# An eight-core encoder layer on Trainium2: local-attention chunks taken one step at a time, one swap in the start-up loads, and twenty extra matmuls in the first loop

## The chip, the cores and the metric

One Trainium2 chip, 8 cores on two dies. Each core computes one of the 8 sequences of the batch; nothing is exchanged between cores. The metric is the device time in microseconds (us) of the slowest core. Engines: PE is TensorE (PEld its weight loads), ACT ScalarE, DVE VectorE, POOL GpSimd, SP SyncE; the last two issue DMAs.

## The reference

```python
h = x @ w_in                                   # 2048 x 1024 by 1024 x 4608
qa, ka, va, za, qb, kb, vb, zb, ga, gb = split(h)
ya = windowed_sink_attention(qa, ka, va, sink) # local: |t-s| <= 128, ALiBi, sink logit
ya = (ya * silu(za)) @ w_proj_a
qh, kh = rope(rms_norm(qb)), rope(rms_norm(kb))
yb = softmax(qh @ kh.T / 8) @ vb               # global, 8 query heads on 2 kv heads
yb = (yb * silu(zb)) @ w_proj_b
y = (sigmoid(ga + b_a) * ya + sigmoid(gb + b_b) * yb) @ w_out
out = layer_norm(2 ** 0.25 * x + y)
```

A sequence has 2048 tokens, the model width is 1024, a head is 64 wide, and each mixer has 8 query heads and 2 key/value heads.

## The kernel before

The tensors that the profile names: `XT` is x transposed in bf16, in four quarters of 512 tokens with 8 slices of 128 channels (k slices, index kc) each. `WS` holds the weights of q, k, v of the global mixer and k, v of the local one; it lies in the memory called `SZ`, so the profile calls it SZ there. `PT` holds exponentiated scores, in 6 slots, a step each. `BIASC` is the local mixer's table of decays (mask included), by which `PT` is multiplied. `G` holds gates, `T` also merged branches and rows of x.

**Start.** DMAs on POOL's queue bring `WS` slice by slice and quarter 0 of `XT` two slices at a time (lines 315 to 328), then the identity and quarter 1 in two halves (330, 331). A DMA that reads the key of an earlier one waits on POOL until that one has landed, so such keys pace the issue. The **first loop** (701 to 705) goes over kc: for blocks 0 to 2 of 128 tokens two matmuls each (384 and 512 columns), then `ka_first` (512 columns). It needs slice kc of both `WS` and `XT`. Then `s_mm(3)` and, for t from 4 to 15, transposes of block t-4 (line 405), the projection of block t, and the rotary and norm work of block t-2 on DVE, ACT and POOL.

**Main loop** (965 to 994). The attention is a list of items (mixer B or A, head pair c, window Q of 512 queries). A B item has 16 steps, one for each block of 128 keys; an A item has 3. A step has score matmuls into a pair of PSUM banks, one exp of 128x1024 on ACT into a `PT` slot, for A one multiply by `BIASC` on DVE, and value matmuls (pv) into bank 4. Two bank pairs alternate, so the scores of step k wait for the exp of step k-2. Sums of the exponentials (ones matmuls) go to bank 5. `batches` packs steps in pairs, a single one where the step is the last of an A item: a B item is 8 batches, an A item a pair and a single.

One turn of the loop, for batch i, writes out this order: scores and exps of further batches, until at least two steps beyond batch i are begun; pv of batch i (and ones, after four steps or at the end of an item); at the end of an item the epilogue's first product `O`; the multiplies by `BIASC` of batch i+1; at the end of an item the transpose `TR`; some **fill** matmuls (`pump`); a tick, at which postponed DVE work runs: one tick after an item's end `rec` (reciprocal, four small copies, transpose `R`), two ticks after it the product into `SZ`. Each engine runs its part of the list in order.

**Fill** is all the rest: projections of local queries, gates and silu paths, the branch projections and the output projection, in groups of 4 or 8 matmuls in banks 6 and 7 alternately, each emptied by ACT or DVE, together with the layer norm. Per window of the loop it has about 176 (first), 320, 352 and 256 matmuls. They are dealt to the batches by weight (lines 863 to 870): 0.9 for a single, 1.5 for a last batch of an item with an A item behind it, 1.0 otherwise. The order of items is B B B A A B A A in window 0, BABABABA in 1, ABABABAB in 2 and 3. Behind the loop the fill of the last window runs by itself, and then the last norm.

Of the kernel before, what the change touches and what calls it, by code (L numbers as in the profile page):

```python
# [170 lines left out]
def build_program():  # L171
# [17 lines left out]
    with contextlib.ExitStack() as es:  # L189
        def sb(name, shape, dt):  # L190
            return es.enter_context(nc.sbuf_tensor(name, shape, dt))

        XT = sb("XT", [128, 4, 8, 512], BF16)
# [31 lines left out]
        PS = es.enter_context(nc.psum_tensor("PS", [128, 8, 512], F32))  # L225
        PSF = PS[:].rearrange("p b f -> p (b f)")

        WS = SZR[:].bitcast(BF16).rearrange("p (k c) -> p k c", k=8)
# [16 lines left out]
        RG_SZ, RG_W, RG_T = ("RG", "SZ"), ("RG", "W"), ("RG", "T")  # L245
# [7 lines left out]
        def pk(b, h=None):  # L253
            return [("PS", b, 0), ("PS", b, 1)] if h is None else [("PS", b, h)]

        def mm(out, lhsT, rhs, start, stop, reads, writes, skip=False):
            s.op("pe", lambda e: e.matmul(out, lhsT=lhsT, rhs=rhs, start=start, stop=stop, skip_group_check=skip),  # L257
                 reads=reads, writes=writes)

        def act(out, in_, func, reads, writes, bias=None, scale=None):  # L260
            kw = {}
            if bias is not None:
                kw["bias"] = bias
            if scale is not None:
                kw["scale"] = scale
            s.op("act", lambda e: e.activation(out=out, in_=in_, func=func, **kw), reads=reads, writes=writes)  # L266
# [8 lines left out]
        def dma(eng, out, in_, reads, writes):  # L275
            s.op(eng, lambda e: e.dma_start(out=out, in_=in_), reads=reads, writes=writes, dma=True)  # L276
# [8 lines left out]
        def load_ws(kc, after=()):  # L285
            dma("pool", WS[:, kc, :], d_ws[:, kc * 1024:(kc + 1) * 1024], [RG_SZ] + list(after), [("WS", kc)])

        def load_xt(n, k0, k1, after=()):
            dma("pool", XT[:, n, k0:k1, :], d_xT[n, :, k0 * 512:k1 * 512].rearrange("p (k t) -> p k t", t=512),
                list(after), [("XT", n, k) for k in range(k0, k1)])  # L290
# [32 lines left out]
        load_ws(4, [("WS", 0)])  # L323
        load_xt(0, 4, 6, [("WS", 1)])
        load_ws(5, [("WS", 2)])
        load_ws(6, [("XT", 0, 2)])
        load_xt(0, 6, 8, [("WS", 3)])
        load_ws(7, [("WS", 4)])
        dma("pool", IDENT[:], d_ident, [], [("IDENT",)])
        load_xt(1, 0, 4, [("WS", 5)])  # L330
        load_xt(1, 4, 8, [("WS", 6)])
        act(ESINK[:], CV[:, 16:20], AF.Exp, reads=[("CV",)], writes=[("ESINK",)])
        s.op("dve", lambda e: e.tensor_scalar_mul(out=CVH[:], in0=CV[:, 0:16], scalar1=0.5),
             reads=[("CV",)], writes=[("CVH",)])
# [9 lines left out]
        def s_part(t, kc, bk, part):  # L344
            n, tt_ = t // 4, t % 4
            xs = XT[:, n, kc, tt_ * 128:(tt_ + 1) * 128]
            rd = [("XT", n, kc), ("WS", kc), RG_SZ]
            if part == 0:
                mm(PS[:, bk, 0:512], xs, WS[:, kc, 0:512], kc == 0, kc == 7, rd, pk(bk))
            elif part == 1:  # L350
                mm(PS[:, bk + 1, 0:384], xs, WS[:, kc, 512:896], kc == 0, kc == 7, rd, pk(bk + 1))
            else:
                mm(PS[:, bk + 1, 384:512], WS[:, kc, 896:1024], xs, kc == 0, kc == 7, rd, pk(bk + 1))
# [6 lines left out]
        def ka_first(kc):  # L360
            mm(PS[:, 4, :], WS[:, kc, 896:1024], XT[:, 0, kc, :], kc == 0, kc == 7,
               [("XT", 0, kc), ("WS", kc), RG_SZ], pk(4))

        def s_copy(t, bk):
            act(VX[:, t, :], PS[:, bk + 1, 128:384], AF.Copy, pk(bk + 1), [("V", t)])
            if t > 3:
                act(KA[:, t * 128:(t + 1) * 128], PS[:, bk + 1, 384:512], AF.Copy, pk(bk + 1), [("KA", t)])
# [333 lines left out]
        for kc in range(8):  # L701
            for t in range(3):
                s_part(t, kc, sbk[t], 1)
                s_part(t, kc, sbk[t], 0)
            ka_first(kc)
        s_copy(0, sbk[0])
        act(KA[:, 0:512], PS[:, 4, :], AF.Copy, pk(4), [("KA", t) for t in range(4)])
        s_copy(1, sbk[1])
# [133 lines left out]
        def make(its):  # L842
            steps = []
            for kind, c, Q in its:
                n = 16 if kind == "B" else 3
                for i in range(n):
                    steps.append(Step(None, kind, c, Q, i, i == n - 1))
            return steps

        def batches(steps):  # L850
            out, i = [], 0
            while i < len(steps):
                n = 1 if steps[i].last else 2
                out.append(steps[i:i + n])
                i += n
            return out

        windows = [[("B", 0, 0), ("B", 1, 0), ("B", 2, 0), ("A", 0, 0), ("A", 1, 0), ("B", 3, 0), ("A", 2, 0), ("A", 3, 0)]]
        for Q in range(1, 4):
            windows.append([(kd, c, Q) for c in range(4) for kd in ("BA" if Q == 1 else "AB")])  # L860
        all_b = [(w, bt) for w, its in enumerate(windows) for bt in batches(make(its))]
        
        def weight_of(i):
            bt = all_b[i][1]
            if len(bt) == 1:
                return 0.9
            return 1.5 if i + 1 < len(all_b) and all_b[i + 1][1][0].kind == "A" and bt[-1].last else 1.0

        weights = [weight_of(i) for i in range(len(all_b))]
        left_b = [sum(x for x, (w, _) in zip(weights, all_b) if w == k) for k in range(4)]  # L870

        def start_batch(bt):
# [210 lines left out]
```

How the kernel before makes its waits and increments, by code:

```python
        def run_stream(e, engobj):  # L116
            waited = {}
            def wait(semkey, sem, val):
                if waited.get(semkey, 0) >= val:
                    return
                waited[semkey] = val
                engobj.wait_ge(sem, val)
            for o in streams[e]:
                for d in o.deps:
                    p = ops[d]
                    if p.dma:
                        wait(("d",) + p.dsem, dsems[p.dsem[0]][p.dsem[1]], p.dval)
                    elif self._need_sync(p, o):
                        wait(("e", p.eng), esem[p.eng], p.cnt)
                if o.dma:
                    sem = dsems[o.dsem[0]][o.dsem[1]]
                    if o.dval > 16:
                        wait(("d",) + o.dsem, sem, o.dval - 16)
                    o.fn(engobj).then_inc(sem, 16)
                else:
                    ins = o.fn(engobj)
                    if o.signal:
                        ins.then_inc(esem[e], 1)
            if e in DMA_POOL:
                last = {}
                for o in streams[e]:
                    if o.dma:
                        last[o.dsem] = o.dval
                for k, v in last.items():
                    wait(("d",) + k, dsems[k[0]][k[1]], v)
```

## Time and profile before

| | us |
|---|---|
| median of 3 runs (lowest, highest) | 697.12 (695.37, 737.5) |
| the profiled execution: its time | 696.03 |
| its span, slowest core (all cores) | 694.5 (690.5 to 694.5) |
| PE, ACT, DVE, POOL busy | 615.0, 391.8, 371.9, 125.4 |

All rows are of core 1, its slowest. Times count from the span's start. A bracket behind a line of a timeline tells how long the engine stood idle before it and what ended that.

### The profile page before, as it was taken

To read this page: it belongs to the slowest core of one execution; us is meant where nothing else is said; L and a number is where in the kernel's file an instruction comes from. 1 tells how busy PE (TensorE), PEld (TensorE's weight loads), DVE (VectorE), ACT (ScalarE), POOL (GpSimd) and SP (SyncE) were. 2 spreads that over 40 slices of the span, in tenths; PEclk is the share of its full clock that TensorE was granted. 3 is DMA by queue.
4 is the path that set the end of the run, shared out by engine and by line. 5 is a ranking of instruction groups with operands and counts; after the bars stand their busy time and mean duration, and the time that the engine had idled before them with its cause. 6 is when DMAs were issued, how large, how long until landed. Compare 5 with 4: busy or idle time off the path is not lost.

```text
span 694.5 us, 13589 instructions; the slowest of 8 cores (690.5 to 694.5 us)
## 1 busy us (share of the span) xinstructions
PE 615.0 (89%) x4440; PEld 237.7 (34%) x4440; DVE 371.9 (54%) x740; ACT 391.8 (56%) x515; POOL 125.4 (18%) x193
## 2 busy tenths in 40 slices
PE   3799988997989999999699799989897999999991
PEld 1356532332333333333233233333332333344440
DVE  2288833326281626265926626174758253579467
ACT  0156678784866566766356275756674767631210
POOL 3268541010011111001111111001110101112012
PEclk9999999998999999999999899999999999999996
DMA  9969739564046432344672543245674224418403
GB/s 136 148 119 126 87 70 157 87 119 58 1 47 107 61 49 39 41 59 76 79 148 49 97 77 48 40 62 92 127 178 103 50 33 61 62 39 202 63 1 121
DMA packets 26772, 57.60 MB, mean 83 GB/s; under 512 B 3024, under 2 KB 5200, under 8 KB 26448
## 3 DMA queue, kind: packets, MB, share of 16 engines
q0 software_dynamic: 21520, 39.36, 41.7%
q1 hardware_dynamic: 5184, 17.38, 7.8%
q8 instruction: 37, 0.61, 0.4%
q14 instruction: 31, 0.25, 0.1%
HBM read 86.65 MB, written 8.39 MB: 137 GB/s over the span
## 4 chain that ended last, share of the span: by engine, by line
PE 73%; DVE 9%; issue 7%; ACT 5%; DMA 4%; POOL 1%; DVEq 0%; ACTq 0%; POOLq 0%
PE PS L257 73%; ACT PT L266 4%; DMA SZ<-ws 2%; DVE PT L269 2%; DMA XT<-xT 1%; DVE T L272 1%; ACT G L266 1%; DVE D L827 1%; DVE WR L269 1%; DVE G L272 1%; DVE STT L574 1%; DVE TR L816 1%; PE PS L405 1%; DVE QB L272 1%; DVE O L269 0%
## 5 line engine op out<-in xcount | busy, mean ns | idle before, releaser
L266 ACT ACTIVATE PT<-PS 128x1024 bf16<-128x1024 f32 (+1 forms) x304 | 292.1, 1018 | 118.4 <-PE PS L257 116.5
L257 PE MATMUL PS<-XT,WROT 128*128 128x512 bf16 x896 | 224.7, 388 | 7.3 <-DVE G L272 6.3
L257 PEld LDWEIGHTS PS<-XT,WROT 128*128 128x128 bf16 x896 | 79.2, 99 | 127.3 <-issue 53.6
L276 POOL DMA_DIRECT2D WROT<-wg x100 | 53.4, 536 | 321.5 <-PE PS L257 320.0
L257 PE MATMUL PS<-PT,VX 128*64 128x512 bf16 (+3 forms) x688 | 97.8, 370 | 9.9 <-DVE PT L269 8.8
L257 PE MATMUL PS<-QB,KB 64*128 64x512 bf16 x512 | 83.6, 387 | 19.2 <-ACT PT L266 18.8
L272 DVE SCALAR_TENSOR_TENSOR G<-G,PS 128x512 f32<-128x512 f32 x64 | 43.0, 681 | 99.2 <-PE PS L257 82.0
L266 ACT ACTIVATE G<-PS,CVH 128x512 f32<-128x512 f32 x64 | 44.1, 689 | 69.7 <-PE PS L257 66.0
L257 PE MATMUL PS<-SZ,XT 128*128 128x384 bf16 (+1 forms) x256 | 58.2, 373 | 15.6 <-DMA XT<-xT 15.5
L257 PE MATMUL PS<-SZ,WR 128*128 128x512 bf16 x256 | 65.7, 383 | 5.7 <-ACT G L266 3.3
L257 PE MATMUL PS<-WR,T 128*128 128x512 bf16 x256 | 60.7, 380 | 0.3 <-DVE T L269 0.2
L272 DVE SCALAR_TENSOR_TENSOR SZ<-G,PS 128x512 bf16<-128x512 f32 x32 | 21.8, 681 | 53.8 <-ACT G L266 29.5
L257 PEld LDWEIGHTS PS<-PT,VX 128*64 128x64 bf16 x688 | 25.9, 109 | 70.5 <-issue 69.8
L257 PE MATMUL PS<-PT,ONES 128*32 128x256 bf16 (+1 forms) x1216 | 48.6, 278 | 0.0
L269 POOL TENSOR_TENSOR SM<-SM,NHALF 128x1 f32<-128x1 f32 x16 | 13.8, 861 | 182.6 <-DVE SM L583 169.4
L257 PEld LDWEIGHTS PS<-QB,KB 64*128 64x128 bf16 x512 | 18.6, 94 | 76.5 <-issue 75.6
L269 DVE TENSOR_TENSOR O<-PS,SZ 128x512 f32<-128x512 f32 x32 | 22.0, 688 | 40.5 <-PE PS L257 40.0
L257 PEld LDWEIGHTS PS<-SZ,XT 128*128 128x128 bf16 x256 | 24.9, 102 | 38.5 <-issue 22.4
L269 POOL TENSOR_TENSOR WR<-WR 128x320 f32<-128x320 f32 x32 | 32.9, 1050 | 23.5 <-DVE WR L269 23.4
L266 ACT ACTIVATE G<-PS 128x512 f32<-128x512 f32 x32 | 19.2, 599 | 31.5 <-PE PS L257 29.3
L257 PEld LDWEIGHTS PS<-SZ,WR 128*128 128x128 bf16 x256 | 22.8, 98 | 39.3 <-issue 16.8
L257 PEld LDWEIGHTS PS<-PT,ONES 128*32 128x32 bf16 x1216 | 25.3, 96 | 30.3 <-issue 29.9
(68 smaller groups left out, 454.9 us busy)
## 6 DMA issues: line engine op xcount, KB each, us to landing
WROT<-wg POOLq DMA_DIRECT2D x100, 256.0 KB, 7.3
T<-x SPq DMA_DIRECT2D x8, 512.0 KB, 4.6
out<-T SPq DMA_DIRECT2D x8, 512.0 KB, 4.2
QB<-x SPq DMA_DIRECT2D x6, 512.0 KB, 7.5
out<-QB SPq DMA_DIRECT2D x6, 512.0 KB, 3.6
SZ<-ws POOLq DMA_DIRECT2D x8, 256.0 KB, 9.3
XT<-xT POOLq DMA_DIRECT2D x2, 1024.0 KB, 9.4
WR<-wo POOLq DMA_DIRECT2D x8, 256.0 KB, 18.2
```

The lines of the kernel that those rows point to most:

```text
L257: s.op("pe", lambda e: e.matmul(out, lhsT=lhsT, rhs=rhs, start=start, stop=stop, skip_group_check=skip), reads=reads, writes=writes)
L266: s.op("act", lambda e: e.activation(out=out, in_=in_, func=func, **kw), reads=reads, writes=writes)
L269: s.op(eng, lambda e: e.tensor_tensor(out=out, in0=in0, in1=in1, op=op), reads=reads, writes=writes)
L272: s.op("dve", lambda e: e.scalar_tensor_tensor(out=out, in0=in0, scalar=scalar, in1=in1, op0=op0, op1=op1), reads=reads, writes=writes)
L276: s.op(eng, lambda e: e.dma_start(out=out, in_=in_), reads=reads, writes=writes, dma=True)
L405: s.op("pe", (lambda o_, i_: lambda e: e.transpose(o_, i_, IDENT[:]))(o_, i_), reads=[("QO", i), ("IDENT",), RG_W], writes=pk(bk))
L574: s.op("dve", lambda e: e.bn_stats(out=STT[:, st, 6 * h:6 * h + 6], in_=xh), reads=[("XB", i, h), rg], writes=[("STT", st, h)])
L816: s.op("dve", lambda e: e.transpose(out=TR[:, k, :], in_=PS[:, YBK, 0:256]), reads=pk(YBK), writes=[("TR", k)])
L827: s.op("dve", (lambda q, f, o: lambda e: e.tensor_copy(out=D[32 * q:32 * q + 32, k, f, :], in_=D[32 * o:32 * o + 32, k, f, :]))(q, f, o), ...
```

## The change

Four edits. In the start-up loads slices 6 and 7 of quarter 0 and slice 6 of the weights change places, and the two halves of quarter 1 wait for weight slices 6 and 7 instead of 5 and 6. In the first loop, for kc from 2 to 6, four matmuls of 512 columns are added behind `ka_first`; they write bank 5, and nothing reads them. `batches` makes a single of every A step and a pair of every two B steps, so an A item is three batches. All batches weigh 1.0.

```diff
-        load_ws(6, [("XT", 0, 2)])
-        load_xt(0, 6, 8, [("WS", 3)])
+        load_xt(0, 6, 8, [("XT", 0, 2)])
+        load_ws(6, [("WS", 3)])
         load_ws(7, [("WS", 4)])
         dma("pool", IDENT[:], d_ident, [], [("IDENT",)])
-        load_xt(1, 0, 4, [("WS", 5)])
-        load_xt(1, 4, 8, [("WS", 6)])
+        load_xt(1, 0, 4, [("WS", 6)])
+        load_xt(1, 4, 8, [("WS", 7)])
...
             ka_first(kc)
+            if 1 < kc < 7:
+                for _ in range(4):
+                    mm(PS[:, 5, :], WS[:, 0, 0:128], XT[:, 0, 0, :], True, True,
+                       [("XT", 0, 0), ("WS", 0), RG_SZ], pk(5))
...
-                n = 1 if steps[i].last else 2
+                n = 1 if steps[i].kind == "A" else 2
...
-        def weight_of(i):
-            bt = all_b[i][1]
-            if len(bt) == 1:
-                return 0.9
-            return 1.5 if i + 1 < len(all_b) and all_b[i + 1][1][0].kind == "A" and bt[-1].last else 1.0
-
-        weights = [weight_of(i) for i in range(len(all_b))]
+        weights = [1.0 for _ in all_b]
```

## Rows read from the trace of the kernel before

**Rows 1.** The page's first lines: span; busy us (share), instructions.
```profile
span 694.5 us, 13589 instructions; the slowest of 8 cores (690.5 to 694.5 us)
PE 615.0 (89%) x4440; PEld 237.7 (34%) x4440; DVE 371.9 (54%) x740; ACT 391.8 (56%) x515; POOL 125.4 (18%) x193
```
**Rows 2.** What PE waited for, whole run: total us, times, longest.
```profile
PE PS L257 <- ACT PT L266: 22.7, 32, 1.4
...
PE PS L257 <- DVE PT L269: 8.8, 8, 2.4
PE PS L257 <- DVE G L272: 8.5, 6, 3.4
```
**Rows 3.** PE timeline: first, a long one and last of sixteen such waits.
```profile
156.02 0.40 PE L257 MATMUL PS<-QA,KA 64*128 64x256 bf16 x4 [1.15 <-ACT PT L266]
...
163.09 0.39 PE L257 MATMUL PS<-QB,KB 64*128 64x512 bf16 x2 [1.38 <-ACT PT L266]
...
589.35 0.39 PE L257 MATMUL PS<-QB,KB 64*128 64x512 bf16 x2 [0.89 <-ACT PT L266]
```
**Rows 4.** All engines' timeline around an A item of window 1.
```profile
260.46 0.62 PE L257 MATMUL PS<-PT,ONES 128*32 128x256 bf16 x16
260.71 0.69 DVE L269 TENSOR_TENSOR O<-PS,SZ 128x512 f32<-128x512 f32 x1 [0.97 <-PE PS L257]
261.02 2.33 PE L257 MATMUL PS<-XT,WROT 128*128 128x512 bf16 x10
261.41 1.29 DVE L269 TENSOR_TENSOR PT<-PT,BIASC 128x1024 bf16<-128x1024 bf16 x2
...
264.04 2.86 ACT L266 ACTIVATE PT<-PS 128x1024 bf16<-128x1024 f32 x3
...
265.16 0.69 DVE L269 TENSOR_TENSOR PT<-PT,BIASC 128x1024 bf16<-128x1024 bf16 x1
265.21 0.39 PE L257 MATMUL PS<-QB,KB 64*128 64x512 bf16 x2 [1.10 <-ACT PT L266]
```
**Rows 5.** DVE timeline around an A item of window 0.
```profile
189.56 0.69 DVE L269 TENSOR_TENSOR O<-PS,SZ 128x512 f32<-128x512 f32 x1 [2.41 <-PE PS L257]
...
194.00 0.65 DVE L269 TENSOR_TENSOR PT<-PT,BIASC 128x1024 bf16<-128x1024 bf16 x1
```
**Rows 6.** PE timeline: longest wait for a multiply, a bank wait in a 1.5 batch.
```profile
345.50 0.41 PE L257 MATMUL PS<-PT,VX 128*64 128x384 bf16 x4 [2.36 <-DVE PT L269]
...
454.54 1.89 PE L257 MATMUL PS<-XT,WROT 128*128 128x512 bf16 x8 [1.45 <-DVE G L272]
```
**Rows 7.** Busy us (x instructions) by stretch; granted clock third from the end.
```profile
160.00:170.00 10.00, 6.45 (x43) 2.29 (x42) 6.00 (x15) 4.05 (x5) 0.00 (x0) 0.79 0.40 52
...
390.00:400.00 10.00, 8.36 (x44) 2.48 (x45) 4.47 (x7) 3.70 (x5) 0.00 (x0) 0.66 0.63 138
...
520.00:530.00 10.00, 6.12 (x46) 2.31 (x44) 8.93 (x21) 2.64 (x3) 1.66 (x3) 1.00 0.38 54
617.00:677.00 60.00, 59.77 (x278) 27.01 (x277) 41.53 (x71) 12.66 (x18) 11.24 (x14) 1.00 0.42 88
```
**Rows 8.** PE timeline of the first loop and the first transposes.
```profile
22.79 2.40 PE L257 MATMUL PS<-SZ,XT 128*128 128x384 bf16 x6 [3.35 <-DMA XT<-xT]
...
27.63 1.29 PE L257 MATMUL PS<-SZ,XT 128*128 128x384 bf16 x6 [0.50 <-DMA XT<-xT]
...
35.50 0.44 PE L405 MATMUL PS<-IDENT,WR 128*128 128x128 bf16 x5 [1.98 <-DVE WR L269]
```
**Rows 9.** POOL's DMA issues; the second's KB, us to landing; all early XT landings.
```profile
18.29 0.53 POOL L276 DMA_DIRECT2D XT<-xT  x1 [0.79 <-DMA SZ<-ws]
...
26.80 0.53 POOL L276 DMA_DIRECT2D XT<-xT  x1 [0.69 <-DMA SZ<-ws]
...
XT<-xT POOLq DMA_DIRECT2D x1, 512.0 KB, 8.0
...
DMA to landing us min/median/max: 6.1/9.0/12.6
```

## The prediction

> **What bounds the kernel now.** I read the page's engine totals first. PE is busy 615.0 of 694.5 us, ACT and DVE a little over half [rows 1]. PE is the engine to look at, and what a change can bring lies in its idle time and its clock. Second, the waits of PE by releaser: 22.7 us for exps, 8.8 for the `BIASC` multiplies, 8.5 for fill banks that DVE empties [rows 2]. Third, the timeline of PE, to see where the exp waits stand. Sixteen of them, from 156.02 to 589.35, are long, 0.89 to 1.38 us, and each of the 16 A items has exactly one; I add them to 17.7 us [rows 3]. The others in that line are some 0.2 us and belong to B batches. Fourth, all engines around one A item, to see how the wait arises [rows 4]. Last, busy time and clock by stretches [rows 7]: PE's clock stands at its upper level (1.00, 2.4 GHz) nearly everywhere, but partly at 0.50 (1.2 GHz) where long waits have come close together. Seven stretches of 10 us show less than 0.95, two of them here. One minus their clock, times 10 us, adds to 11.9 us of lost full-speed time.
>
> **How the A wait arises.** Behind the pair A0, A1 the loop finds nothing begun, so it begins the single A2 and then the next pair: three steps of scores in a row. With two bank pairs the third waits for the exp of A2, issued just before it. The row shows ACT with three exps in a line, 2.86 us from 264.04, and PE idle 1.10 us before the third scores [rows 4].
>
> **Part 1, single A steps.** In the new order the turn of A0 begins A2 alone; the turn of A1 begins the next pair, whose second step needs A2's exp, by then a whole turn old; the turn of A2 begins nothing. No turn issues three scores. The 16 waits go: -17.7 us.
>
> The price is in the multiplies. A0 and A1 were multiplied together, ahead of `rec`. Now A1's multiply is issued one turn later, behind `rec`, and pv of A1, with the fill behind it, waits for it. I follow the item of [rows 4]. DVE: `O` at 260.71, the two multiplies to 262.7, then `TR` and `rec`, and at 265.16 the next multiply of 0.69. With one multiply of 0.65 less ahead, A1's would end at 265.85 - 0.65 = 265.2. PE: ones 0.56; fill of 7.3 matmuls at 0.217 (10 in 2.17 us), 1.6; scores of A2 0.2; pv of A0 0.3; fill 1.6; scores of a pair 0.5: pv of A1 is reached at 260.46 + 4.8 = 265.3. Wait about nil. In window 0 the fill is 4.0 a batch, 0.87 us, so PE arrives 1.5 us sooner against its `O`, and DVE, from `O` at 189.56 to the multiply's end at 194.65 less one short multiply of 0.6, is done at 194.0 [rows 5]. PE, 0.25 us ahead of its `O` there as above, would come at 189.3 + 3.3 = 192.6: wait 1.4 us in each of 4 items, 5.6 us. For the 12 others I take 0.5 us, since normalisation work and bank emptying lie in DVE's queue at some of them: 6.0. Together 11.6 against 8.8 now: +2.8. Below, the bound is the first item's nil for all twelve, 5.6 us in all, -3.2. Above, every item at 1.4 us, 22.4, +13.6.
>
> **Part 2, equal weights.** The fill's matmuls are the same, dealt otherwise. The weights of window 1 sum to 32 + 2 + 7.6 = 41.6 now and to 44 then, so a B batch gets 320/44 = 7.3 instead of 7.7, and the batch ahead of A 7.3 instead of 11.5. The bank wait of 1.45 us at 454.54 stands in such a 1.5 batch [rows 6], where DVE has `O` and two multiplies ahead of the bank. Such waits should mostly go, but DVE is busy 8.93 of 10 us at 520 to 530 [rows 7]; where DVE is the slower engine a saved PE wait comes back as a bank wait. I take these as even: 0, between -3 (two such waits) and +4 (one more of the longest, 3.4 us [rows 2]). In window 0, B batches pace themselves by the exp with waits of about 0.2 us; 0.33 matmul less, 0.07 us over some 32 batches, makes at most +2.3. I take +1.5, and 0 as the lower end.
>
> **The clock.** With the exp waits gone (the longest, 1.38 us at 163.09 [rows 3], stands in the low stretch from 160) some low stretches go. Of the 11.9 us [rows 7] I take a third, -4, since the new waits of window 0 may keep theirs: between 0 and -10.
>
> Here a rule of the Trainium skill speaks against a denser PE. TensorE: Matmul & The Clock Gate (Part 1) says that a peak-current limiter takes a die to 13/16 of the clock once three of its cores run dense matmuls. The trace does not agree: from 617 to 677, PE is busy 59.77 of 60 us with all eight cores at the same work, at a clock of 1.00 [rows 7].
>
> **Part 3, twenty matmuls.** In the first loop PE waits 3.35 us at 22.79 and 0.50 at 27.63 for `XT` [rows 8]. Four matmuls at 0.213 are 0.85 us a slice. Those of kc 2 and 3 fall into the first wait, which shrinks to about 1.7 us: free. Those of kc 4 lie before the landing that kc 5 needs. If the shorter gap keeps the clock up, kc 4 takes 1.4 us instead of 2.6, kc 5 still starts at about 25.5 (its weight slice releases POOL at 25.6), its four end at 27.8 and kc 6 starts 0.2 late. Those of kc 6 lie under nothing, as kc 7's weights are there: 0.85. Sum +1.05; if the clock falls all the same, one more slow slice, +2.1. Nothing behind gives it back: the rotary chain on DVE starts from kc 7 and PE waits for it until 35.50 [rows 8], and after 40 us PE is never idle till 82.
>
> **Part 4, the loads.** kc 6 needs both swapped pieces; the same two issue slots, 16.97 and 18.29, carry both, the later at 18.29 [rows 9], and its piece lands at 27.5 [rows 8] in either order: 0. The halves of quarter 1 are issued when weight slices 6 and 7 have landed, 27.5 and 28.8 instead of 25.58 and 26.80 [rows 9]. With the 8.0 us of the second half [rows 9] it lands at 36.8; the block that reads it comes directly behind the transposes at 35.50, 1 us later then, and needs its fifth slice about 1.2 us on, near 38: covered by 1 us. Without cover, at the longest landing of an early `XT` piece (12.6 us [rows 9]), it would cost up to 3.4; I take 0. On POOL's queue the identity stands ahead, and behind the halves come the rotary additions from 31.46; POOL is free at 29.4, so they are not late.
>
> **Sum.** -17.7 + 2.8 + 0 + 1.5 - 4 + 1.05 = -16.4 us, against the profiled execution's own 696.0 (span 694.5 and 1.5 around it): 679.6. The median of the runs is 1.1 above it, so 681.
>
> **Rivals.**
> **A, the forecast:** 681, with its own range of 673 to 689 from the clock's and the multiplies' bounds. For it: the cause is written out in the order of scores, and the waits are the same in all 16 items. Chance 0.60.
> **B, the wait moves to DVE.** A1's multiply behind `rec` delays pv everywhere as in window 0: 22.4 us of such waits, no clock back. -17.7 + 13.6 + 1.5 + 1.05 = -1.6: 696. For it: DVE is near full around A items of window 3 [rows 7]; against it: at 265 the times meet, and less fill ahead of `rec` means fewer banks to empty there. Chance 0.22.
> **C, all goes well:** multiplies -3.2, banks -3, clock -10, 0 for the B batches: -17.7 - 3.2 - 3 - 10 + 1.05 = -32.9, 664. Halfway from A, 672, is the likely case of this kind. Chance 0.10.
> **D, slower.** pv of A1 waits as long in each item as the longest wait for a multiply now, 2.36 us [rows 6]: 37.8 us, +29.0; with +1.5 and +1.05 the sum is +13.9, 711. It decides against the change once the waits for multiplies pass 8.8 + 17.7 - 2.6 = 23.9 us, 1.5 an item. Little speaks for it outside window 0. Chance 0.05.
> **E, the denser PE is granted less clock.** If the dense stretch of 60 us ran at the 0.79 of 160 to 170 [rows 7], it would take 76 us, 16 more: 697. Chance 0.03. The rule above gives 13/16 for it.
>
> **How the numbers follow.** A measurement of this kernel can tell about 2%, 14 us, from no change: below 683.2 is faster. Of A's 0.60 some 0.45 lies there, and C's 0.10: faster 0.55. The rest of A, B, E and half of D: same 0.42. Slower 0.03. The range of 671 to 695 leaves out part of C, the upper end of B and D, together some 0.2.
>
> **What would show each step.** Right: PE's waits for exps fall from 22.7 to 5 to 7 us, and no pv or score row has 0.9 us or more for an exp. Waits for multiplies total 6 to 15 us, at the second pv of an A item, longest in window 0. The transposes of 35.50 come at 36.5. Wrong: waits for multiplies above 20 us, or bank waits above 12 (DVE the bound); a DMA wait at the first use of quarter 1; more low-clock stretches than seven.

## The result: 689.1 us, 1.1% faster, less than half of the forecast gain

| | before | changed |
|---|---|---|
| median, us | 696.74 | 689.12 |
| ratio (95% interval) | | 0.989 (0.986 to 0.992) |
| profiled execution: span of the slowest core | 694.5 | 686.1 |
| mean span of the eight cores | 692.1 | 682.5 |

Each side ran four times, once in a slower state of the chip (737.5 and 722.8 us); the ratio is that of the fast runs alone.

The change saves 7.6 us where 16 were forecast. The time lies in the range of 671 to 695, but outside A's own of 673 to 689 by a hair, and within the 2% called "same", which had 0.42 against 0.55 for faster.

The profile of the changed kernel, its slowest core (6). First the head of the page: span, then busy us (share of the span) and instructions. It answers [rows 1].

```profile
span 686.1 us, 13648 instructions; the slowest of 8 cores (678.9 to 686.1 us)
...
PE 617.3 (90%) x4460; PEld 237.4 (35%) x4460; DVE 372.3 (54%) x740; ACT 390.6 (57%) x515; POOL 126.0 (18%) x193
```

What PE waited for (total us, times, longest), which answers [rows 2]:

```profile
PE PS L257 <- DVE PT L269: 23.3, 19, 2.5
PE PS L257 <- DMA XT<-xT: 14.9, 3, 13.3
PE PS L257 <- ACT PT L266: 6.4, 18, 1.0
...
PE PS L257 <- DVE G L272: 1.8, 3, 0.9
PE PS L257 <- DVE O L269: 1.4, 2, 0.9
...
PE PS L257 <- ACT G L266: 1.2, 3, 0.6
```

The exp waits went as forecast, 22.7 to 6.4. Multiply waits went from 8.8 to 23.3 and took nearly all of it back. And the bank waits, `G` by DVE and ACT together, fell from 11.8 to 3.0, which the sum had at nothing. Two large terms were wrong in opposite directions; that the time lies in the stated range all the same is owed to that, and is luck.

To see where time goes in all runs alike I made one account for each of them: over the main loop (88 to 620 us), PE's waits by cause, and the lost full-speed time by stretches of 10 us as in the prediction (90 to 620 us), both as means over the eight cores. "mult" is a wait for a `BIASC` multiply, "bank" one for `G`, "O" one for the first product of an epilogue.

| kernel | ratio to before | mean span | exp | mult | bank | O | clock |
|---|---|---|---|---|---|---|---|
| before | 1 | 692.1 | 23.0 | 8.8 | 12.0 | 0.2 | 9.8 |
| changed | 0.989 | 682.5 | 6.5 | 23.8 | 3.2 | 1.4 | 5.1 |
| E1 main loop edits only | 0.9864 | 681.1 | 6.5 | 23.5 | 3.2 | 1.5 | 6.4 |
| E2 start edits only | 1.0027 | 693.9 | 22.9 | 8.8 | 12.0 | 0.3 | 9.8 |
| E8 equal weights only | 0.9884 | 685.1 | 23.1 | 10.8 | 7.3 | 0.4 | 4.3 |
| E9 single steps, old weights | 1.0088 | 697.2 | 5.2 | 29.0 | 7.2 | 1.0 | 17.3 |
| E3 changed + early multiplies | 0.9689 | 670.0 | 6.4 | 5.2 | 9.1 | 4.6 | 1.1 |
| E4 changed + late `rec` | 0.9871 | 682.3 | 6.1 | 24.1 | 2.0 | 1.4 | 7.0 |
| E5 E3 without start edits | 0.9662 | 670.3 | 6.4 | 5.2 | 9.0 | 4.6 | 2.2 |
| E10 E5 with old weights | 0.9807 | 678.8 | 5.2 | 7.9 | 11.7 | 7.3 | 5.1 |
| E11 E5, A steps at 0.63 | 0.9733 | 674.0 | 4.2 | 9.2 | 9.5 | 6.9 | 3.2 |
| E12 E5 + late `rec` | 0.9648 | 668.0 | 6.1 | 0.4 | 8.1 | 10.0 | 3.8 |

The account is not exact: a wait at the low clock counts twice, and the start is not in it. From before to changed its main-loop terms sum to -13.8 and the mean span moved by -9.6; the start, below, explains some 2 of the difference, and about 2 stay unexplained. From before to E9 it gives +5.9 for +5.1, to E8 -7.9 for -7.0, but to E5 -26.4 for -21.8: a sum of its terms can be off by 2 to 5 us.

Half of the interval of each ratio is 0.0010 to 0.0020 (for the changed kernel 0.003).

### The profile page after: what moved, and what is told of

It reads as the page before. It is cut to its first block, busy times and chain, and to the rows that moved or that the text cites. A ratio compares the mean times of both kernels' runs of the same rounds, so it can differ in the third digit from the quotient of the medians.

```text
span 686.1 us, 13648 instructions; the slowest of 8 cores (678.9 to 686.1 us)
## 1 busy us (share of the span) xinstructions
PE 617.3 (90%) x4460; PEld 237.4 (35%) x4460; DVE 372.3 (54%) x740; ACT 390.6 (57%) x515; POOL 126.0 (18%) x193
## 4 chain that ended last, share of the span: by engine, by line
PE 76%; DVE 8%; issue 5%; DMA 5%; ACT 4%; DVEq 0%; POOL 0%; ACTq 0%; POOLq 0%
PE PS L257 75%; DMA SZ<-ws 4%; ACT PT L266 3%; DVE PT L269 2%; DMA XT<-xT 1%; ACT G L266 1%; DVE D L831 1%; DVE WR L269 1%; PE PS L405 1%; DVE QB L272 0%; DVE TR L820 0%; DVE STT L574 0%; DVE G L272 0%; DVE O L269 0%; DVE T L272 0%
## 5 line engine op out<-in xcount | busy, mean ns | idle before, releaser
L257 PE MATMUL PS<-XT,WROT 128*128 128x512 bf16 x896 | 222.2, 384 | 2.0 <-DVE G L272 1.8
L257 PE MATMUL PS<-PT,VX 128*64 128x512 bf16 (+3 forms) x688 | 100.0, 368 | 25.9 <-DVE PT L269 23.3
L257 PEld LDWEIGHTS PS<-XT,WROT 128*128 128x128 bf16 x896 | 77.6, 98 | 116.8 <-issue 42.9
L257 PE MATMUL PS<-QB,KB 64*128 64x512 bf16 x512 | 80.9, 383 | 6.2 <-ACT PT L266 5.8
L269 POOL TENSOR_TENSOR WR<-WR 128x320 f32<-128x320 f32 x32 | 32.8, 1048 | 23.3 <-DVE WR L269 23.3
L257 PEld LDWEIGHTS PS<-PT,ONES 128*32 128x32 bf16 x1216 | 25.4, 96 | 30.2 <-issue 29.9
L269 DVE TENSOR_TENSOR WR<-PS,T 128x512 f32<-128x512 f32 (+1 forms) x64 | 26.8, 482 | 15.0 <-PE PS L257 15.0
L257 PEld LDWEIGHTS PS<-SZ,WR 128*128 128x128 bf16 x256 | 23.1, 99 | 34.0 <-issue 11.5
```

The source lines that it names most:

```text
L269: s.op(eng, lambda e: e.tensor_tensor(out=out, in0=in0, in1=in1, op=op), reads=reads, writes=writes)
```

## The experiments

Edits are shown against the changed kernel.

### What the two halves of the change do: E1 and E2

**E1**, the main loop's edits alone: both load edits undone and the extra matmuls left out.

```diff
-        load_xt(0, 6, 8, [("XT", 0, 2)])
-        load_ws(6, [("WS", 3)])
+        load_ws(6, [("XT", 0, 2)])
+        load_xt(0, 6, 8, [("WS", 3)])
...
-            if 1 < kc < 7:
-                for _ in range(4):
...
```

> The changed kernel with the loads of the kernel before and without the twenty extra matmuls: only the main loop's edits are left. My reading now: the main loop gained about 10 us (exp waits 22.7 to 6.4 us, bank waits 11.8 to 3.0, multiply waits 8.8 to 23.3) and the start lost about 2.6 (transposes 1.3 us later, up to 1.3 us of DMA wait at quarter 1). Then this kernel takes 686.5 us, 10 below the kernel before. Rival: the extra matmuls and the swapped loads cost nothing or help (the clock stays up in the start); then 689 to 691.

Measured: 0.9864 (0.9846 to 0.9883), 686.0 us beside 695.8 of the kernel before: 9.8 us gained. The three wait totals are those of the changed kernel.

**E2**, the start's edits put into the kernel before.

> The kernel before with the start's edits alone (swapped loads, later quarter 1, twenty extra matmuls). If the start costs 2.6 us: 699.3 us, a DMA wait of about 1 us at the first use of quarter 1 on some cores, the first transposes 1.3 us later. Rival, that the start's edits are free: 696.7.

Measured: 1.0027 (1.0017 to 1.0038), 698.2 us; by the ratio that is +1.9 us (1.2 to 2.6). Four of the eight cores wait 0.66 to 1.22 us for quarter 1. So the start's edits cost about 2 us, and the main loop's gain is about 10, not 16.

### What takes the exp waits' place: E3 and E4

This is the changed kernel around an A item of window 3, on core 6. All engines' timeline, start, us, engine, instruction:

```profile
514.28 0.62 PE L257 MATMUL PS<-PT,ONES 128*32 128x256 bf16 x16
514.52 0.69 DVE L269 TENSOR_TENSOR O<-PS,SZ 128x512 f32<-128x512 f32 x1
...
515.73 0.44 DVE L820 STREAM_TRANSPOSE TR<-PS 128x256 f32<-128x256 f32 x1
...
516.77 0.69 DVE L272 SCALAR_TENSOR_TENSOR T<-T,PS 128x512 f32<-128x512 f32 x1 [0.60 <-PE PS L257]
...
517.56 0.69 DVE L574 BATCH_NORM_STATS2 STT<-T 128x6 f32<-128x512 f32 x1
...
518.74 0.24 DVE L827 RECIPROCAL D<-TR 128x16 f32<-128x16 f32 x1
...
519.93 0.71 DVE L834 STREAM_TRANSPOSE R<-D 128x512 f32<-128x512 f32 x1
520.57 0.65 DVE L269 TENSOR_TENSOR PT<-PT,BIASC 128x1024 bf16<-128x1024 bf16 x1
...
521.36 0.64 PE L257 MATMUL PS<-PT,VX 128*64 128x256 bf16 x4 [2.51 <-DVE PT L269]
```

The multiply of A1 begins at 520.57, 6.1 us behind `O`. Ahead of it in DVE's queue stand, first, the emptying of an output-projection bank, for which DVE itself stands idle 0.60 us since PE has not filled the bank yet; then 2 us of that and of the norm's statistics; then the reciprocal work, 1.8 us. PE has nothing that it could do in the 2.51 us: its queue is as strictly in order.

**E3** puts every multiply into the turn in which its scores are begun. The multiply of A1 moves one turn up by this, ahead of `rec`.

```diff
             for st in bt:
                 st.exp()
+            unscaled.extend(bt)
...
-            for st in all_b[i + 1][1] if i + 1 < len(all_b) else ():
-                st.bias()
+            while unscaled:
+                unscaled.pop(0).bias()
```

> The changed kernel with every BIASC multiply issued in the turn in which its scores are begun, so those of A0 and A1 stand together ahead of the reciprocal work, as in the kernel before. Theory (the second multiply behind the reciprocal work ate the gain): the wait at the second pv of an A item, 18 us in all, goes; multiply waits fall from 23.3 to under 8 us and the time to about 678. Rival (DVE is the bound around an A item whatever the order): multiply waits fall, but waits for banks, O and the third multiply rise by the same, and the time stays within 3 us of 689.

Measured: 0.9689 (0.9676 to 0.9703), 674.2 us, 2% below the changed kernel's ratio. PE's waits on its slowest core:

```profile
PE PS L257 <- DVE G L272: 8.4, 10, 2.2
PE PS L257 <- ACT PT L266: 6.4, 18, 1.0
PE PS L257 <- DVE PT L269: 5.2, 7, 1.4
PE PS L257 <- DVE O L269: 4.9, 5, 1.5
```

The same item in its timeline:

```profile
502.02 0.69 DVE L269 TENSOR_TENSOR O<-PS,SZ 128x512 f32<-128x512 f32 x1 [0.45 <-PE PS L257]
502.63 1.28 DVE L269 TENSOR_TENSOR PT<-PT,BIASC 128x1024 bf16<-128x1024 bf16 x2
...
506.05 0.41 PE L257 MATMUL PS<-PT,VX 128*64 128x256 bf16 x4
...
509.22 1.02 PE L257 MATMUL PS<-SZ,WR 128*128 128x512 bf16 x4 [2.22 <-DVE G L272]
```

Both multiplies are done at 503.9 and the second pv, at 506.05, has no wait. The order in DVE's queue was the cause: the theory holds. The rival holds for a part of it. Multiply waits fell by 18.6 us, bank and `O` waits rose by 9.1, as at 509.22: around such an item DVE really has too much to do. The ratio fell by 2%, 14 us, and the mean span by 12.5, more than the 9.5 us of waits saved; the clock gives most of the rest, 5.1 us lost in the changed kernel, 1.1 with early multiplies. It is also 4 us better than the 678 expected, which had no term for the clock. The stretch of 10 us with the lowest clock on the slowest core of the changed kernel, and the same stretch in E3 (busy us by engine; the clock is the third number from the end):

```profile
170.00:180.00 10.00, 8.16 (x57) 2.44 (x61) 6.77 (x15) 5.52 (x7) 0.00 (x0) 0.68 0.02 3
```

```profile
170.00:180.00 10.00, 9.07 (x77) 2.94 (x77) 5.77 (x14) 7.55 (x10) 0.00 (x0) 1.00 0.01 2
```

**E4** leaves the multiplies where the changed kernel has them and puts `rec` and the final product a tick later.

```diff
-            later(1, rec)
-            later(2, final)
+            later(2, rec)
+            later(3, final)
```

> The changed kernel with the reciprocal work and the final product of each item one tick later; the multiply of A1 then stands ahead of it, that of A2 behind it or next to it. Theory: the wait at the second pv goes, some of it comes back at the third: 680 to 683. Rival (DVE is the bound): 687 to 690.

Measured: 0.9871 (0.9851 to 0.9892), 686.4 us, between the two expectations. The multiply waits did not turn into bank waits (2.0 us), as the rival had it. The theory expected some of them to come back at the third pv, and nearly all did: they total 24.1, beside 23.8 in the changed kernel, and moved one step on. PE's timeline in windows 0 and 2, core 2:

```profile
202.32 0.64 PE L257 MATMUL PS<-PT,VX 128*64 128x384 bf16 x4 [2.13 <-DVE PT L269]
...
211.27 0.41 PE L257 MATMUL PS<-PT,VX 128*64 128x384 bf16 x4 [2.81 <-DVE PT L269]
...
389.25 0.41 PE L257 MATMUL PS<-PT,VX 128*64 128x384 bf16 x4 [2.00 <-DVE PT L269]
```

128x384 in the pv of A2 marks the third step. `rec` now stands ahead of A2's multiply. With a single step in a batch a multiply is issued just one turn ahead of its use, and whichever of them stands behind `rec` is late.

### What the start costs: E5, E6, E7

All three have early multiplies, so that the main loop does not disturb the comparison. **E5** has neither start edit, **E6** only the extra matmuls, **E7** only the load edits.

```diff
 E5, E6 (where the swap of lines 326 and 327 is undone too):
-        load_xt(1, 0, 4, [("WS", 6)])
-        load_xt(1, 4, 8, [("WS", 7)])
+        load_xt(1, 0, 4, [("WS", 5)])
+        load_xt(1, 4, 8, [("WS", 6)])
...
 E5, E7:
-            if 1 < kc < 7:
-                for _ in range(4):
...
```

> The changed kernel with early multiplies, and with neither of the start's edits. Earlier multiplies alone took 0.9689 of the time before, the start's edits added 0.27% to the kernel before. If the two add up: 0.9662 of the time before, 672.3 us; no DMA wait at quarter 1, first transposes about 35.5. Rival: the start's edits cost only where the main loop loses clock anyway; then no difference, 0.969.

> Early multiplies, the loads of the kernel before, the twenty extra matmuls kept. If the later issue of quarter 1 costs what its DMA waits show (0.5 to 1.9 us on half of the cores, the slowest ones): 0.967 of the time before, 673, and no wait at quarter 1; the first transposes stay 1 us late. Rival: the extra matmuls are the whole cost, 0.969.

> Early multiplies, the swapped and later loads kept, no extra matmuls. If the extra matmuls cost the 1.05 us worked out for them: 0.9675; PE idle about 3.3 us again before slice 4, transposes at about 35.5, and the DMA wait at quarter 1 longer by the same 1 us, which would take the gain back: then 0.969. Rival, that they pay by keeping the clock up: slower than 0.969.

Measured: E5 0.9662 (0.9647 to 0.9677), E6 0.9676 (0.9662 to 0.9691), E7 0.9693 (0.9679 to 0.9706). E5 and E6 came out as expected. E7 is the case in which a longer wait for quarter 1 takes back what the missing matmuls save: five of its cores wait 0.29 to 2.93 us there, and without the load edits no core waits there in E5 or E6.

So the load edits alone cost 0.0031, about 2.2 us, and the extra matmuls alone 0.0014, about 1 us. The first is at the edge of what the intervals separate, the second below it. The two do not add up: with both (E3, 0.9689) it is 0.0027 over E5, as in E2. The extra matmuls let PE come later to quarter 1 and so hide a part of the load edits' cost: in E3 four cores wait there, 0.52 to 1.94 us; beside the matmuls (E3 less E6) that is 0.0013, about 0.9 us. The traces bear out the sum: the first scores of the main loop begin at 85.4 us in the mean of the four kernels with both edits (changed, E2, E3, E4) and at 83.8 in the eight with neither. In E5 PE waits again 2.3 to 4.2 us before slice 4 on the cores, and loses nothing by it that the ratio shows.

In the changed kernel this is the place, PE's timeline and POOL's issues of quarter 1 on core 6, with the landing of the two (KB each, median us), which answer [rows 8, 9]:

```profile
23.82 1.29 PE L257 MATMUL PS<-SZ,XT 128*128 128x384 bf16 x6 [0.27 <-DMA XT<-xT]
...
37.31 0.44 PE L405 MATMUL PS<-IDENT,WR 128*128 128x128 bf16 x5 [1.98 <-DVE WR L269]
37.59 0.81 PE L257 MATMUL PS<-SZ,XT 128*128 128x384 bf16 x4
39.68 1.35 PE L257 MATMUL PS<-SZ,XT 128*128 128x384 bf16 x4 [1.28 <-DMA XT<-xT]
```

```profile
29.03 0.53 POOL L276 DMA_DIRECT2D XT<-xT  x1 [6.43 <-DMA SZ<-ws]
30.21 0.53 POOL L276 DMA_DIRECT2D XT<-xT  x1 [0.66 <-DMA SZ<-ws]
...
XT<-xT POOLq DMA_DIRECT2D x2, 512.0 KB, 8.5
```

The long wait before slice 4 is filled by the extra matmuls: on core 1, 3.35 us [rows 8] against 0.47 at 22.68 in the changed kernel. Then four matmuls of the first block of quarter 1 run and the fifth, on slice 4, stands 1.28 us for the second half.

The same place on core 4, with the issue of the second half and its own landing:

```profile
28.77 0.53 POOL L276 DMA_DIRECT2D XT<-xT  x1 [0.66 <-DMA SZ<-ws]
XT<-xT POOLq DMA_DIRECT2D x1, 512.0 KB, 10.0
38.90 1.44 PE L257 MATMUL PS<-SZ,XT 128*128 128x384 bf16 x4 [1.15 <-DMA XT<-xT]
```

### What the weights do: E8 to E11

**E8** is the kernel before with all weights 1.0 and its pairs kept.

> The kernel before with all weights 1.0, A steps still a pair and a single. If the weights do little by themselves: exp waits stay at 22.7 us, bank waits (DVE and ACT, 11.8) fall by up to 3, multiply waits rise by up to 3: 0.997 to 1.003 of the time before. Rival, that the equal weights are what emptied the bank waits (11.8 to 3.0 us in the changed kernel): 0.985 to 0.99.

Measured: 0.9884 (0.9871 to 0.9898), 690.0 us. The rival, and clearly: this one edit gives 8 us, as much as the whole change. Bank waits fell by 4.7 us, multiply waits rose by 2.0, and the lost clock halved, 9.8 to 4.3.

**E9** is its counterpart: single steps, with the fill dealt as before. An A item keeps its 1.9.

```diff
+        def weight_of(i):
+            if all_b[i][1][0].kind == "A":
+                return 0.63
+            return 1.5 if i + 1 < len(all_b) and all_b[i + 1][1][0].kind == "A" and all_b[i][1][-1].last else 1.0
```

> Main loop only: single A steps, but the fill dealt as in the kernel before (1.5 for the batch ahead of A, 0.63 for each A step, 1.9 an item). Equal weights alone took the kernel before to 0.9884, and equal weights with single steps to 0.9864. If single steps by themselves bring little because of the second multiply: 0.995 to 1.00, exp waits 6 us, multiply waits above 20, bank waits above 8. Rival, that single steps and weights overlap (each alone brings the same gain): about 0.988.

Measured: 1.0088 (1.0076 to 1.0101), 702.3 us: worse than both expectations. The edit that takes the exp waits away makes the kernel slower by itself. PE's waits, and the clock of two stretches, on core 2:

```profile
PE PS L257 <- DVE PT L269: 30.1, 20, 3.2
...
PE PS L257 <- ACT PT L266: 5.1, 16, 0.8
```

```profile
200.00:210.00 10.00, 8.00 (x58) 2.37 (x55) 6.38 (x15) 4.58 (x5) 1.59 (x3) 0.67 0.19 27
500.00:510.00 10.00, 9.11 (x52) 2.49 (x54) 5.32 (x12) 4.07 (x5) 0.00 (x0) 0.66 1.04 254
```

The exp waits fell by 17.8 us, multiply waits rose by 20.2 and the lost clock by 7.5. Two reasons for the multiplies can be read from the order: a large share of fill in the turn ahead of A means that more banks are emptied ahead of `rec`, and the short A turns bring PE to the next pv sooner. I did not test the two apart.

**E10** and **E11** deal the fill differently with early multiplies and no start edits: E10 with E9's weights, E11 with A steps at 0.63 and all else 1.0.

> As the last, with early multiplies. With equal weights this was 0.9662. If the weights' gain is the bank waits behind the 1.5 batch and the clock they cost: 0.972 to 0.976, bank waits above 10 us. Rival, that once no multiply is late the weights no longer matter: 0.966.

> Early multiplies, single steps, no start edits; A steps weigh 0.63, all else 1.0. Less fill beside the A steps means fewer banks for DVE to empty there, but shorter turns. If what is left (bank waits 7.8, O waits 4.6, multiply waits 5.2) is DVE having too much in too short a time, shorter turns make it worse: 0.970 to 0.975. Rival, that the banks emptied there are the load: 0.962 to 0.966.

Measured: E10 0.9807 (0.9789 to 0.9824), E11 0.9733 (0.9718 to 0.9749), against 0.9662 with equal weights. E11 lies in the range expected of DVE having too much in too short a time; E10 is worse than its 0.972 to 0.976. Even with the multiplies early, DVE needs the time: with 0.63 for an A step the waits of the columns mult, bank and O together rise from 18.8 to 25.6 us, and with 1.5 ahead of A the bank waits grow by another 2.2. Equal weights give an A item 3.0 shares of fill instead of 1.9. My reading of this is that PE then has more work beside which DVE can do what the item and its neighbour ask of it.

### The fastest version: E12

**E12** is E5 with E4's edit.

> Early multiplies and the reciprocal work one tick later. If the order in DVE's queue is all that matters, nothing of A now stands behind the reciprocal work except the third multiply: as without, 0.966, within 0.003. If the reciprocal work still holds up O and the banks at the end of an item (4.6 and 7.8 us): 0.960 to 0.963.

Measured: 0.9648 (0.9634 to 0.9661), 671.6 us beside 696.1. Multiply waits are all but gone (0.4), `O` waits doubled to 10.0 and the rest is about even. This meets the first of its two expectations, the ratio of E5 within 0.003. It beats both kernels, the changed one by 2.4% in the ratios; over E5 the gain is within the intervals, and `rec` has only moved its waits once more.

## Why the prediction was wrong, point by point

**What bounds the kernel, and how the A wait arises: right.** All 16 long exp waits are gone, no row of 0.9 us or more for an exp is left around an A item (the one of 1.0 stands in the first batches). -17.7 and +1.5 were forecast for the exps, -16.5 was measured. The two edits apart show the cause: with pairs kept (E8) the exp waits stay at 23.1 us, with single steps (E9) they are 5.2.

**Part 1, the price in the multiplies: the step that failed.** The sum had +2.8, with +13.6 as the upper bound; it was +15.0. In window 0 the working held: 5.6 us forecast at the second pv, 1.42 + 1.47 + 1.49 + 1.61 = 6.0 measured. The failure is "for the 12 others I take 0.5 us". On the slowest core the second pv waits 0.38, 1.09, 2.31, 1.10, 0.99, 2.39, 2.51 and 1.80 us in eight of them, 12.6 in all, not 6.0. And first and third pv waits, which had no term, add 4.7; so the total passes even the upper bound. The item of [rows 4], on which the twelve rested, is one of the four without a wait, and it happens to be free of output projection and norm. In the changed kernel, too, its second pv comes without a wait, behind a multiply at 270.20:

```profile
266.37 0.62 PE L257 MATMUL PS<-PT,ONES 128*32 128x256 bf16 x16
266.61 0.69 DVE L269 TENSOR_TENSOR O<-PS,SZ 128x512 f32<-128x512 f32 x1 [0.56 <-PE PS L257]
...
270.20 0.65 DVE L269 TENSOR_TENSOR PT<-PT,BIASC 128x1024 bf16<-128x1024 bf16 x1
...
271.36 0.41 PE L257 MATMUL PS<-PT,VX 128*64 128x256 bf16 x4
```

From `O` to the end of that multiply it is 4.2 us here, 4.5 as forecast, and 6.7 in the item at 514.52. DVE's rows around a heavy item of before were there to be read: 8.93 busy of 10 us at 520 to 530 [rows 7]. I quoted them and did not put them in the sum.

**Part 2, equal weights: wrong in size.** Taken as "even, 0", between -3 and +4; the bank waits fell by 8.8 us. E8 gives the edit alone: -4.7 in bank waits, +2.0 in multiply waits, -5.5 in lost clock. The other half belongs to Part 1, which had no term for it: with single steps and the old weights (E9) the bank waits fall by 4.7 too. The bank wait that I had named, 1.45 us in a 1.5 batch [rows 6], pointed the right way: E10, with 1.5 ahead of A again, has 2.7 us more of them than E5. Their sum over such batches was not worked out.

**The clock: right in size, -4.7 for -4, but by luck.** It was ascribed to the exp waits. E8 has all of these and loses only 4.3 us; E9 has none of the long ones and loses 17.3. Where the loss changes most, it goes with waits for DVE: with the bank waits from before to E8 (12.0 to 7.3), with the multiply waits from E3 or E5 to E9 (5.2 to 29.0). No run changes one kind of wait alone, so which of them brings the clock down is not shown.

**Part 3, the extra matmuls: right.** +1.05 forecast; 0.0014 of the time, 1.0 us, was measured with a wide interval. The first transposes come 1.3 us later as a mean over cores (35.45 to 36.76 us); with early multiplies and the new loads the matmuls move them by 0.7 (E7 35.50, E3 36.22).

**Part 4, the loads: wrong, though small.** Forecast 0, "covered by 1 us", at most 3.4; measured about 0.9 us beside the extra matmuls and 2.2 without them. Two figures of core 1 failed on the others. One is the issue: I took the landing of weight slice 7, 28.8, that is 2.0 us later than before. In the changed kernel the second half is issued 1.8 to 4.6 us later than before on the same core, 2.9 in the mean; on core 6 at 30.21 instead of 25.62. The other is the 8.0 us to landing: on the four cores that wait (0.49 to 1.28 us) it took 8.6 to 10.0, on the four that do not 6.9 to 8.1. Core 4 issues at 28.77, exactly as forecast, and still waits 1.15 us, as its half takes 10.0 to land. This wait at the first use of quarter 1 was named as a sign against the prediction. The landings of before, 7.7 to 9.4 us over the eight cores, were there to be read. A cover of 1 us, read from one core, does not hold for the slowest of eight.

**Rivals.** B was the closest: "the wait moves to DVE", +13.6 for the multiplies against +15.0 measured, at 0.22. It erred in giving no clock back and in leaving the bank waits where they were. E9 shows the slower side that rival D described: multiply waits of 29.0 us, above the 23.9 worked out as the point of no gain, and the kernel is slower. There the mechanism was in the change all along, and the equal weights, taken as nothing, kept it from deciding. E, the denser PE granted less clock, did not come: behind the loop of the changed kernel PE is again full at the upper level, and in E3, where PE's waits are among the fewest (25.4 us in the four columns, beside 42.4 in E9), 1.1 us of clock is lost, the least of all. The dense stretch, answering the last of [rows 7]:

```profile
620.00:630.00 10.00, 10.00 (x49) 4.50 (x47) 8.77 (x14) 0.69 (x1) 4.13 (x6) 1.00 0.87 171
```

The limiter's 13/16, which the Trainium skill names for three busy cores of a die (TensorE: Matmul & The Clock Gate, Part 1), does not stand in this row either.

**Where the expected gain went:** of 16.4 us, 12.2 more than forecast went to multiplies, most of them behind `rec`, 1.2 to `O`, about 0.9 to the loads of quarter 1; 8.8 came back from the bank waits and 1.0 from exps and clock. That leaves 11.9 us, against 9.6 in mean span and 7.6 in the medians. So some 2 us stay unexplained in the mean and 4 in the medians, of which 1.2 is that the slowest core stands 3.6 us above the mean span instead of 2.4.

## What to carry to other kernels

Finer steps take a wait from one engine and tighten the deadline on another: before splitting a batch, list for each piece what stands ahead of it in the queue of every engine that it uses, at the heaviest place and not at a clean one, and issue short work with a near deadline (here 0.65 us) ahead of long work with a far one (1.8 us). An edit that "deals the same work otherwise" needs a term of its own; here it was worth as much as the whole change. And where the time is that of the slowest of eight cores, a cover counts only if it holds on all of them.

## What the runs showed of the hardware that was not expected

The clock answers to waits with more than their own length. From E5 to E9, which differ by early multiplies and weights, the waits of the four kinds (exps, multiplies, banks, `O`) grow by 17.2 us, 25.2 to 42.4, the mean span by 26.9, and the lost clock by 15.1. A single long wait does not always lower it: behind the 2.51 us at 521.36 the stretch of 520 to 530 stands at 0.83, but on the slowest core of E3 no stretch of the main loop is below 1.00 though PE waits 2.22 us at 509.22. What decides between the two no run here shows.
